# Paged attention: half of the pages fetched by rows on GpSimd, transposes alternating between two pairs of banks, and the prompt's value sums of two heads interleaved

## The chip, the cores and the metric

The kernel runs on one core of one Trainium2 chip. The metric is the device time in microseconds of one execution; before the change the median of three runs is 2847.95 us (2846.03 to 2848.89). TensorE is called PE, VectorE DVE, ScalarE ACT, GpSimd POOL and SyncE SP in the profile. Everything is computed in float32.

## What is computed

The reference is one inference step of a two-layer decoder trunk, for a prompt of 1024 tokens and 8 sample sequences of 4 new tokens each (32 tokens), with a mixture of experts after each layer. The first layer holds a gated convolution and a recurrent block, the second a convolution module and a latent attention with 8 heads. The change lies in that attention. With keys and values in one latent of 256 numbers per position and a rotary key of 32, the reference is

```
s = einsum('bthr,bsr->bhts', q_lat, ckv) + einsum('bthp,bsp->bhts', q_pe, kpe)
s = where(k_pos <= q_pos, s * SCALE, -inf)
p = softmax(s)                      # over the positions s
o_lat = einsum('bhts,bsr->bthr', p, ckv)
y = einsum('bthr,rhv->bthv', o_lat, w_uv)
```

For the prompt, s runs over 1024 positions, causally. For a sample sequence it runs over 4096 past positions, which lie in a cache as 32 pages of 128 rows in an order given by a page table, and over its 4 new positions. A cache row is 288 numbers: 256 of the latent and 32 of the rotary key, 1152 bytes.

## The kernel before

Every engine has its own program, written out by hand, and the programs meet only in semaphores; each engine runs its instructions in the written order. The stages follow one another: first layer, experts, second layer's projections (`*_odd`), prompt attention (`*_prompt`), paged attention (`*_sample`), output projection, experts.

**Prompt attention.** Heads go in pairs: two iterations of a loop with two pairs (`a`, `pp`), so four rounds. A round projects queries, keys and values of a pair (lines 1263 to 1275) and then works through 16 units u = 2t + j: block t of 128 queries, head j of the pair. `scores(u)` multiplies against (t+1)·128 keys, into PSUM banks 0/1 or 2/3 by the parity of u. DVE masks and takes the maximum (`maximum`), ACT takes the exponential (`expo`), DVE divides (`divide`), PE transposes the t+1 blocks of the probabilities into banks 4/5 (`turn`), ACT copies these to SBUF (`stage`; one place for each head, the tiles cosq and sinq), and `weigh(u)` multiplies them with the values (line 1253). The output of head 0 lies in PSUM partitions 0 to 63, that of head 1 in 64 to 127, of bank 6 or 7 by the parity of t. PE's order in step u is scores(u+1), turn(u-1), weigh(u-2). One product of 128·128 with 128·64 is one `matmul` in the source and two instructions in the profile.

**Paged attention.** There are two places for pages, `kv[0]` (the tile xT) and `kv[1]`; sequence b lies in place s = b mod 2. SP loads a sequence as four quarters h of 8 pages. For each page it reads the physical page number from the table and issues one DMA of 128 rows (`load_quarter`, lines 1384 and 1385). The semaphore d_pv, which PE raises after each quarter of the old sequence has been weighed, frees a quarter's place, and SP waits for it at line 1403.

`body(b, s)` on each engine does the scores of sequence b and finishes sequence b-1 between them. There are ten turns for a sequence. Turns 0 and 5 transpose the rotary keys of half the pages, which POOL has copied together (`rotary_keys`, line 1562; it waits for both quarters of its half). Turns 1 to 4 and 6 to 9 transpose four pages each, eight transposes into PSUM banks 0 and 1; ACT copies bank 0 and DVE bank 1 to SBUF (`take`, lines 1595 and 1646). Turn k waits until both copies of turn k-1 are done (lines 1437 and 1438). PE's order in a body is: turns 0 and 1, the transpose of the row maxima (1477), turn 2, the matmul that spreads the bias (1482), turns 3 and 4, the eight transposes of the probabilities of b-1 (1493, also into banks 0 and 1) and their sums, scores(0), turn 5, weigh(0), turn 6, weigh(1), turn 7, weigh(2), turn 8, weigh(3), turn 9, and scores(4). The scores go to banks 2/3 or 4/5 by s. Each weigh is 8 pages. POOL's order is: for each later sequence, wait for the scores, fill the queries, and then the two rotary copies of its halves (`both`).

Before the first body PE waits for two weights and forms the latent queries of all sequences (lines 1416 to 1425, banks 3 to 5), ACT and DVE copy them out, and DVE spreads the rotary queries (lines 1629 to 1636).

**Gathers elsewhere.** POOL gathers rows with indirect DMAs in the experts (line 726, 128 rows of 2 KB; the index column is copied first, line 722) and in the FFN's end (line 876, 128 rows of 4 KB).

Of the kernel before, what the change touches and what calls it, by code (L numbers as in the profile page):

```python
# [53 lines left out]
C_ID, C_ONE, C_TRI, C_IOTA, C_IOTA4, C_TOK, C_VALID, C_CAUSAL, C_NEW, C_FOLD, C_ROW, C_LOW, C_HALF, C_N = 0, 128, 256, 384, 400, 404, 422, 431, 559, 815, 943, 1071, 1199, 1200  # L54
# [27 lines left out]
def build(nc, io):  # L82
    ctx = contextlib.ExitStack()
    with ctx:
# [59 lines left out]
        pages = sb("pages", [1, SEQS * PAGES], I32)  # L144
        with contextlib.ExitStack() as st:
# [17 lines left out]
            with contextlib.ExitStack() as st2:  # L163
# [9 lines left out]
                nmax, nms, den, rden = (sb(n, [P, 2]) for n in ("nmax", "nms", "den", "rden"))  # L173
# [799 lines left out]
        def sp_odd(sp):  # L973
            w_in = io["w_in_odd"].rearrange("(k p) n -> p k n", p=P)
            for dst, src in ((odp[:], io["od_pack"]), (gqk[:], io["gqk"]), (cosq[:], io["cosq"]), (sinq[:], io["sinq"]),
                             (wuv[:], io["wuv"].rearrange("(k p) n -> p k n", p=P)), (pages[:], io["page_table"])):
                sp.dma_start(dst, src).then_inc(sem("in_odd"), 16)
# [151 lines left out]
        def dve_odd(dve, D):  # L1129
# [94 lines left out]
        def pe_prompt(pe):  # L1224
# [22 lines left out]
            def weigh(u, u0, t0):  # L1247
                t, j = divmod(u, 2)
                pe.wait_ge(sem("a_pt"), 1 + u0 + u + 1)
                if j == 0:  # L1250
                    pe.wait_ge(sem("a_yt"), t0 + t + 1)
                for b in range(t + 1):
                    ins = nc.tensor.matmul(PS[V_DIM * j:V_DIM * (j + 1), 6 + t % 2, 0:P], V[:, b, V_DIM * j:V_DIM * (j + 1)], PT[u % 2][:, b, :],  # L1253
                                           start=(b == 0), stop=(b == t))
                ins.then_inc(sem("a_v"), 1)

            with pe.Fori(0, 2) as a:
                for pp in range(2):
# [19 lines left out]
                    for u in range(18):  # L1278
                        if u + 1 < 16:
                            scores(u + 1, u0)  # L1280
                        if 0 <= u - 1 < 16:
                            turn(u - 1, u0)
                        if 0 <= u - 2 < 16:
                            weigh(u - 2, u0, t0)

        def act_prompt(act, A):
# [18 lines left out]
            def result(t, a, pp, u0):  # L1305
                act.wait_ge(sem("a_v"), u0 + 2 * t + 2)
# [73 lines left out]
        ROUND = [1, 2, 3, 4, 6, 7, 8, 9]  # L1380

        def load_quarter(sp, b, s, h):
            for n in range(h * 8, h * 8 + 8):
                phys = sp.value_load(pages[0:1, bass.ds(b * PAGES + n, 1)], min_val=0, max_val=io["cache"].shape[0] // PAGE - 1)  # L1384
                sp.dma_start(page(s, n), io["cache"][bass.ds(phys * PAGE, PAGE), :]).then_inc(sem(f"in_kv{s}{h}"), 16)  # L1385
# [5 lines left out]
        def sp_sample(sp):  # L1391
            for h in range(4):
                load_quarter(sp, 0, 0, h)
# [4 lines left out]
            for h in range(4):  # L1398
                load_quarter(sp, 1, 1, h)
            with sp.Fori(0, 3) as i:  # L1400
                for s in range(2):
                    for h in range(4):
# [12 lines left out]
        def pe_sample(pe):  # L1415
            pe.wait_ge(sem("in_attn_w"), 64)

            for r in range(2):
                for h in range(HEADS):
                    ins = nc.tensor.matmul(PS[:, 4 + r, h * SAMPLE:(h + 1) * SAMPLE], wukT[h // 4][:, h % 4, r * P:(r + 1) * P], qns[:, h, :], start=True, stop=True)  # L1420
            ins.then_inc(sem("d_ql"), 1)

            for r in range(2):
                ins = nc.tensor.transpose(PS[0:SAMPLE, 3, r * P:(r + 1) * P], ckvT[:, r, PROMPT:TOK], ident)
            ins.then_inc(sem("d_ql"), 1)

            def body(b, s, first, last):
                sb_ = 2 + 2 * s

                def turn(k):  # L1430
# [6 lines left out]
                    pe.wait_ge(sem("d_cta"), b * 10 + k)  # L1437
                    pe.wait_ge(sem("d_ctd"), b * 10 + k)
                    part(pe)
                    if q is None:  # L1440
                        for n in range(4):
                            ins = nc.tensor.transpose(PS[:, n // 2, n % 2 * P:n % 2 * P + P], kpr[:, k // 5, n, :, :].rearrange("p a b -> p (a b)"), ident)
                    else:
                        for n in range(8):
                            ins = nc.tensor.transpose(PS[:, n // 4, n % 4 * P:n % 4 * P + P], page(s, 4 * q + n % 4)[:, n // 4 * P:(n // 4 + 1) * P], ident)  # L1445
                    ins.then_inc(sem("d_t"), 1)

                def scores(q0):
# [3 lines left out]
                    bank = sb_ + q0 // 4  # L1452
# [25 lines left out]
                if not last:  # L1478
                    turn(2)
                if not first:  # L1480
# [6 lines left out]
                if not first:  # L1487
                    pe.wait_ge(sem("d_e"), b * 2)
                    if not last:
                        pe.wait_ge(sem("d_cta"), b * 10 + 5)  # L1490
                        pe.wait_ge(sem("d_ctd"), b * 10 + 5)
                    for n in range(8):
                        nc.tensor.transpose(PS[:, n // 4, n % 4 * P:n % 4 * P + P], Pd[:, n * P:(n + 1) * P], ident)
# [54 lines left out]
        def pool_sample(pool):  # L1548

            CP = nc.gpsimd.tensor_copy  # L1550
            pool.wait_ge(sem("d_ql"), 1)
# [24 lines left out]
            with pool.Fori(0, 3) as i:  # L1576
                for s in range(2):
                    pool.wait_ge(sem("d_s"), i * 4 + 2 * s + 2)
                    part(pool)
                    fill(i * 2 + 2 + s, s)  # L1580
                    both(i * 2 + 2 + s, s)

        def act_sample(act, A):
            AC = nc.scalar.activation
            act.wait_ge(sem("d_ql"), 1)
            act.wait_ge(sem("d_qp"), 1)
            for r in range(2):
                src = PS[:, 4 + r, 0:HEADS * SAMPLE].rearrange("p (h b t) -> p b h t", h=HEADS, t=STEP)
                AC(qlat[:, r, :, :].rearrange("p b (h t) -> p b h t", t=STEP), src, ACT.Copy).then_inc(sem("d_qa"), 1)

            def body(b, s, first, last):
                def take(k):
                    act.wait_ge(sem("d_t"), b * 10 + k + 1)
                    part(act)
                    ins = AC(CT[ROUND.index(k) % 4][:, 0, :], PS[:, 0, :], ACT.Copy) if k in ROUND else \
# [307 lines left out]
```

## Time and profile before

| | us |
|---|---|
| median of three runs | 2847.95 |
| the profiled execution | 2847.57 |
| its span, first to last instruction | 2845.8 |
| prompt attention, a round (four) | 64.85 |
| paged attention, scores(0) of one sequence to scores(0) of the next | 44.3 to 45.4 |

| engine | busy us | share of the span |
|---|---|---|
| PE | 2343.5 | 82% |
| DVE | 980.7 | 34% |
| ACT | 610.5 | 21% |
| POOL | 325.4 | 11% |

A row of the timeline gives the start in us from the span's start, the duration (of several merged instructions from the first start to the last end), the engine, the line, the operation, output and inputs, partitions and elements, the count, and in brackets how long the engine had been idle and what released it. "issue" means that nothing in the profile explains the idle time. PE's ends are modelled, so start times are read rather than ends. Tiles are shown by the name of the memory: cosq and sinq are the transposed probabilities of the two heads, lngb the probabilities, peT and CT the turned pages, KT the turned rotary keys. The clock column is the granted TensorE clock: 1.00 is 2.4 GHz and 0.50 is 1.2 GHz. DMA is the mean busy share of the 16 DMA engines, and the last number is GB/s.

### The profile page before, as it was taken

To read this page: it belongs to the slowest core of one execution; us is meant where nothing else is said; L and a number is where in the kernel's file an instruction comes from. 1 tells how busy PE (TensorE), PEld (TensorE's weight loads), DVE (VectorE), ACT (ScalarE), POOL (GpSimd) and SP (SyncE) were. 2 spreads that over 40 slices of the span, in tenths; PEclk is the share of its full clock that TensorE was granted. 3 is DMA by queue.
4 is the path that set the end of the run, shared out by engine and by line. 5 is a ranking of instruction groups with operands and counts; after the bars stand their busy time and mean duration, and the time that the engine had idled before them with its cause. 6 is when DMAs were issued, how large, how long until landed. Compare 5 with 4: busy or idle time off the path is not lost.

```text
span 2845.8 us, 41210 instructions
## 1 busy us (share of the span) xinstructions
PE 2343.5 (82%) x13984; PEld 1388.1 (49%) x13985; DVE 980.7 (34%) x1711; ACT 610.5 (21%) x1037; POOL 325.4 (11%) x362
## 2 busy tenths in 40 slices
PE   7999798599999934979799987676897798999850
PEld 4666454355555523645466664444454454555420
DVE  2333333311111154798855442222233311111117
ACT  2222211111111122321344432111111110111112
POOL 0000000000100042742000000000000000001014
PEclk9999899699999966989988887766898799999985
DMA  3112223167677665102000122334424158555845
GB/s 118 38 38 89 87 99 140 59 233 288 230 260 275 221 190 165 37 26 83 22 6 26 46 68 73 100 103 113 146 71 162 32 219 304 219 207 172 306 144 184
DMA packets 175229, 384.45 MB, mean 135 GB/s; under 512 B 16241, under 2 KB 89346, under 8 KB 175154
## 3 DMA queue, kind: packets, MB, share of 16 engines
q1 hardware_dynamic: 146882, 314.31, 31.3%
q0 software_dynamic: 13072, 44.88, 4.9%
q10 hardware_dynamic: 15200, 24.39, 3.2%
q8 instruction: 31, 0.51, 0.1%
q14 instruction: 44, 0.36, 0.0%
HBM read 339.18 MB, written 44.35 MB: 135 GB/s over the span
## 4 chain that ended last, share of the span: by engine, by line
PE 68%; DVE 17%; DMA 4%; issue 4%; SPq 3%; ACT 1%; DVEq 1%; POOL 0%; ACTq 0%; POOLq 0%
PE PS L770 20%; PE PS L783 11%; PE PS L292 10%; PE PS L505 9%; DVE yT L241 5%; PE PS L1237 3%; PE PS L1445 2%; PE PS L1253 2%; DMA w<-in_w_exp_out 2%; DVE yst L241 2%; SPq L1384 2%; SPq L1385 1%; PE PS L778 1%; PE PS L1244 1%; PE PS L1455 1%
## 5 line engine op out<-in xcount | busy, mean ns | idle before, releaser
L770 PE MATMUL PS<-yT,yst 128*64 128x256 f32 x2816 | 315.7, 383 | 22.3 <-DMA w<-in_w_exp_out 22.3
L783 PE MATMUL PS<-w,ht 128*64 128x512 f32 x1312 | 317.8, 605 | 11.5
L292 PE MATMUL PS<-xT,W 128*128 128x352 f32 x960 | 287.8, 463 | 18.1 <-ACTq L301 18.1
L770 PE MATMUL PS<-xT,yst 128*64 128x256 f32 x2432 | 275.0, 385 | 19.2 <-DMA w<-in_w_exp_out 10.7
L770 PEld LDWEIGHTS PS<-yT,yst 128*64 128x64 f32 x2816 | 204.3, 139 | 145.5 <-issue 52.8
L505 PE MATMUL PS<-wo,yst 128*128 128x512 f32 x576 | 257.9, 603 | 17.3 <-POOL yst L483 15.4
L292 PEld LDWEIGHTS PS<-xT,W 128*128 128x128 f32 x960 | 184.2, 192 | 120.1 <-ACTq L301 17.8
L770 PEld LDWEIGHTS PS<-xT,yst 128*64 128x64 f32 x2432 | 177.8, 139 | 127.5 <-issue 47.1
L998 PE MATMUL PS<-xT,W 128*128 128x352 f32 (+1 forms) x672 | 203.2, 466 | 33.7 <-ACT qT L1073 21.6
L998 PEld LDWEIGHTS PS<-xT,W 128*128 128x128 f32 (+1 forms) x672 | 127.2, 190 | 109.5 <-issue 45.4
L505 PEld LDWEIGHTS PS<-wo,yst 128*128 128x128 f32 x576 | 108.8, 193 | 142.7 <-issue 142.7
L817 ACT ACTIVATE sg<-PS 128x128 f32<-128x128 f32 x164 | 45.4, 277 | 592.8 <-PE PS L770 592.4
L833 DVE TENSOR_TENSOR hx<-sg,PS 128x128 f32<-128x128 f32 x164 | 46.4, 283 | 340.1 <-ACT sg L817 340.1
L241 DVE SCALAR_TENSOR_TENSOR yT<-hp,odp,yT x88 | 153.2, 1741 | 16.0 <-DVE yT L241 15.2
L837 DVE COPY ht<-PS 128x128 f32<-128x128 f32 x164 | 47.8, 292 | 321.0 <-PE PS L778 321.0
L726 POOL DMA_INDIRECT yst<-xm,idx x84 | 81.3, 968 | 555.4 <-PE PS L755 544.6
L783 PEld LDWEIGHTS PS<-w,ht 128*64 128x64 f32 x1312 | 79.6, 136 | 121.9 <-issue 70.2
L846 DVE COPY wo<-PS 128x512 f32<-128x512 f32 x82 | 56.7, 692 | 207.9 <-PE PS L783 207.9
L488 PE MATMUL PS<-cst,xn 128*128 128x128 f32 x216 | 38.3, 336 | 82.2 <-POOL xn L887 69.6
L817 ACT ACT_TABLE_LOAD x38 | 48.8, 1283 | 240.4 <-issue 240.4
L1237 PE MATMUL PS<-K,Q 96*128 96x512 f32 (+3 forms) x192 | 90.4, 588 | 7.4 <-ACT lngb L1297 4.5
L584 DVE SCALAR_TENSOR_TENSOR sx<-xres,PS 128x1024 f32<-128x1024 f32 x18 | 22.0, 1221 | 177.8 <-PE PS L505 177.8
(335 smaller groups left out, 2666.8 us busy)
## 6 DMA issues: line engine op xcount, KB each, us to landing
xT<-in_w_exp_in SPq DMA_DIRECT2D x32, 2048.0 KB, 12.8
w<-in_w_exp_out SPq DMA_DIRECT2D x32, 2048.0 KB, 18.2
yT<-in_w_exp_in SPq DMA_DIRECT2D x32, 2048.0 KB, 12.8
yb<-wo ACTq DMA_DIRECT2D x164, 128.0 KB, 2.3
xT<-in_cache SPq DMA_DIRECT2D x128, 144.0 KB, 2.1
kv<-in_cache SPq DMA_DIRECT2D x128, 144.0 KB, 2.1
W<-in_w_in_even SPq DMA_DIRECT2D x20, 512.0 KB, 4.0
xm<-xn SPq DMA_DIRECT2D x18, 512.0 KB, 2.9
```

The source lines that it names most:

```text
L241: return nc.vector.scalar_tensor_tensor(out, x, scalar, acc, ALU.mult, ALU.add)
L292: ins = nc.tensor.matmul(PS[:, n % 5, 0:CW], W5[:, p, k, :], xT[:, k, c * CW:(c + 1) * CW], start=(k == 0), stop=(k == KD - 1))
L505: ins = nc.tensor.matmul(PS[:, (t % 2) * 2 + n, :], yst[:, s, k, :], wo[:, k, n * 512:(n + 1) * 512], start=(k == 0), stop=(k == KD - 1))
L726: pool.indirect_dma_start(out=gx, out_offset=None, in_=xm[l].rearrange("t (h c) -> (t h) c", h=2), in_offset=bass.IndirectOffsetOnAxis(ap= ...
L770: ins = nc.tensor.matmul(PS[cols, 2 + q, 0:2 * P].rearrange("p (g f) -> p g f", g=2), xtb[:, k, :], w[:, k, t, :, q * P:(q + 1) * P], star ...
L783: ins = nc.tensor.matmul(PS[cols, 4, :], ht[:, q, t, :], w2[:, s, 2 * t + q, n * 512:(n + 1) * 512], start=(q == 0 and t == 0), stop=(q == ...
L817: nc.scalar.activation(sg[:, q, :], PS[:, 2 + q, 0:P], ACT.Silu).then_inc(sem(u + "sg"), 1)
L998: ins = nc.tensor.matmul(PS[0:m, (n0 + c) % 6, 0:CW], W4[:, slot, k, 0:m], xT[:, k, c * CW:(c + 1) * CW], start=(k == 0), stop=(k == KD - 1))
L1237: ins = nc.tensor.matmul(PS[:, u % 2 * 2 + c // 512, 0:w], Q[j][:, t * P:(t + 1) * P], K[j][:, c:c + w], start=True, stop=True)
L1253: ins = nc.tensor.matmul(PS[V_DIM * j:V_DIM * (j + 1), 6 + t % 2, 0:P], V[:, b, V_DIM * j:V_DIM * (j + 1)], PT[u % 2][:, b, :], start=(b = ...
L1384: phys = sp.value_load(pages[0:1, bass.ds(b * PAGES + n, 1)], min_val=0, max_val=io["cache"].shape[0] // PAGE - 1)
L1445: ins = nc.tensor.transpose(PS[:, n // 4, n % 4 * P:n % 4 * P + P], page(s, 4 * q + n % 4)[:, n // 4 * P:(n // 4 + 1) * P], ident)
```

## The change

It has three parts.

- **Pages.** The page table is loaded into all 128 partitions, and DVE turns it, at the start of the second layer, into row numbers: page·128 + partition. SP loads quarters 0 and 2 as before. POOL fetches quarters 1 and 3: it copies 8 columns of the row numbers and issues 8 indirect DMAs, each of which gathers 128 rows. In the loop POOL does so after it has filled the queries and before the two rotary copies (`both`). At the start it gathers sequence 0 when the projections have read xT, and sequence 1 when the last prompt result is written, ahead of its first rotary copy.
- **Banks.** Turn k writes banks 0/1 or 4/5 by the parity of k and waits for the copies of turn k-2. The probabilities are transposed into banks 4/5. The scores of both places go to banks 2/3. The latent queries are formed after turn 2 of the first body, in banks 6 and 7, and DVE's rotary queries come after its second copy there.
- **Prompt.** `weigh` takes a block t of both heads at once, alternating between the heads, in the odd steps, ahead of turn(u-1).

Its core (the query part moves as said; ACT and DVE read the new banks):

```diff
-        pages = sb("pages", [1, SEQS * PAGES], I32)
+        pages = sb("pages", [P, SEQS * PAGES], I32)
+        pidx = sb("pidx", [P, 32], I32)
...
+            D(nc.vector.tensor_copy(rtmp[:, 0:SEQS * PAGES], pages[:, :]))
+            D(TS(rtmp[:, 0:SEQS * PAGES], rtmp[:, 0:SEQS * PAGES], float(PAGE), cst[:, C_PART:C_PART + 1], ALU.mult, ALU.add))
+            D(nc.vector.tensor_copy(pages[:, :], rtmp[:, 0:SEQS * PAGES]))
             dve.sem_inc(sem("o_zero"), 1)
...
-            def weigh(u, u0, t0):
-                t, j = divmod(u, 2)
-                pe.wait_ge(sem("a_pt"), 1 + u0 + u + 1)
-                if j == 0:
-                    pe.wait_ge(sem("a_yt"), t0 + t + 1)
+            def weigh(t, u0, t0):
+
+                pe.wait_ge(sem("a_pt"), 1 + u0 + 2 * t + 2)
+                pe.wait_ge(sem("a_yt"), t0 + t + 1)
                 for b in range(t + 1):
-                    ins = nc.tensor.matmul(PS[V_DIM * j:V_DIM * (j + 1), 6 + t % 2, 0:P], V[:, b, V_DIM * j:V_DIM * (j + 1)], PT[u % 2][:, b, :],
-                                           start=(b == 0), stop=(b == t))
+                    for j in range(2):
+                        ins = nc.tensor.matmul(PS[V_DIM * j:V_DIM * (j + 1), 6 + t % 2, 0:P], V[:, b, V_DIM * j:V_DIM * (j + 1)], PT[j][:, b, :],
+                                               start=(b == 0), stop=(b == t))
...
+                        if u >= 3 and u % 2 == 1:
+                            weigh((u - 3) // 2, u0, t0)
                         if 0 <= u - 1 < 16:
                             turn(u - 1, u0)
-                        if 0 <= u - 2 < 16:
-                            weigh(u - 2, u0, t0)
...
+        PAIR = [0, 4]
...
+        def gather_quarter(pool, b, s, h):
+
+            j = s * 16 + h // 2 * 8
+            nc.gpsimd.tensor_copy(pidx[:, j:j + 8], pages[:, bass.ds(b * PAGES + h * 8, 8)]).then_inc(sem("d_ix"), 1)
+            pool.wait_ge(sem("d_ix"), b * 2 + h // 2 + 1)
+            part(pool)
+            for n in range(8):
+                pool.indirect_dma_start(out=page(s, h * 8 + n), out_offset=None, in_=io["cache"],
+                                        in_offset=bass.IndirectOffsetOnAxis(ap=pidx[:, j + n:j + n + 1].bitcast(U32), axis=0)
+                                        ).then_inc(sem(f"in_kv{s}{h}"), 16)
...
             with sp.Fori(0, 3) as i:
                 for s in range(2):
-                    for h in range(4):
+                    for h in (0, 2):
                         sp.wait_ge(sem("d_pv"), i * 8 + (4 * s + h + 1))
                         load_quarter(sp, i * 2 + s + 2, s, h)
...
-                    pe.wait_ge(sem("d_cta"), b * 10 + k)
-                    pe.wait_ge(sem("d_ctd"), b * 10 + k)
+                    if not first or k >= 2:
+                        pe.wait_ge(sem("d_cta"), b * 10 + k - 1)
+                        pe.wait_ge(sem("d_ctd"), b * 10 + k - 1)
                     part(pe)
+                    bank = PAIR[k % 2]
...
                 if not last:
                     turn(2)
+                if first:
+                    queries()
...
         def pool_sample(pool):
-            pool.wait_ge(sem("d_ql"), 1)
+            pool.wait_ge(sem("o_zero"), 1)
+            pool.wait_ge(sem("o_mm"), 1 + 9 + 42)
+            for h in (1, 3):
+                gather_quarter(pool, 0, 0, h)
+            pool.wait_ge(sem("a_yt"), 2 + 32)
+            pool.wait_ge(sem("a_qns"), 8)
+            for h in (1, 3):
+                gather_quarter(pool, 1, 1, h)
...
                     fill(i * 2 + 2 + s, s)
+                    for h in (1, 3):
+                        pool.wait_ge(sem("d_pv"), i * 8 + (4 * s + h + 1))
+                        gather_quarter(pool, i * 2 + s + 2, s, h)
                     both(i * 2 + 2 + s, s)
```

## Rows read from the trace of the kernel before

**Rows 1.** Stretches: length, busy us (instructions) PE, PEld, DVE, ACT, POOL; clock, DMA.

```profile
1476.96:1541.81 64.85, 61.66 (x323) 41.75 (x323) 31.66 (x85) 29.27 (x60) 0.00 (x0) 0.92 0.02 6
1625.50:1634.50 9.00, 9.00 (x24) 4.73 (x23) 4.57 (x15) 3.54 (x10) 0.00 (x0) 0.50 0.00 0
1780.00:1825.90 45.90, 31.21 (x272) 20.68 (x268) 10.14 (x23) 7.76 (x16) 1.66 (x4) 0.69 0.38 104
1799.50:1825.50 26.00, 15.95 (x68) 11.06 (x72) 5.86 (x16) 4.87 (x10) 1.66 (x4) 0.50 0.42 115
```

**Rows 2.** Timeline, one sequence: start, us, engine, line, operation, count, idle before.

```profile
1782.57 1.07 PE L1465 MATMUL PS<-kv,lngb 128*32 128x256 f32 x16
1784.52 37.57 SPq L1385 DMA_DIRECT2D kv<-in_cache  x32
1804.93 0.61 POOL L1562 COPY kpr<-kv 128x512 f32<-128x512 f32 x1 [25.07 <-DMA kv<-in_cache]
1805.79 1.09 PE L1442 MATMUL PS<-cst,kpr 128*128 128x128 f32 x4 [10.72 <-POOL kpr L1562]
1808.70 0.15 DVE L1658 TENSOR_TENSOR mxd<-mxd,mxn 32x1 f32<-32x1 f32 x1
1819.13 1.94 PE L1493 MATMUL PS<-cst,lngb 128*128 128x128 f32 x8 [0.99 <-DVE peT L1646]
1822.18 1.07 PE L1455 MATMUL PS<-CT,qb 128*32 128x512 f32 x2
```

**Rows 3.** A row of the chain; then the timeline of a round's end.

```profile
1603.41 3.26 PE PS L1253 x32
...
1594.94 1.98 PE L1237 MATMUL PS<-K,Q 96*128 96x512 f32 x4
1600.75 1.02 ACT L1303 ACTIVATE cosq<-PS 128x1024 f32<-128x1024 f32 x1 [0.64 <-PE PS L1244]
1604.81 0.27 PE L1253 MATMUL PS<-cosq,V 128*64 128x128 f32 x1
1604.87 0.27 PE L1253 MATMUL PS<-sinq,V 128*64 128x128 f32 x1
1606.60 5.59 PE L1263 MATMUL PS<-qT,wqn 128*128 128x352 f32 x18
```

**Rows 4.** Timeline of GpSimd, first FFN stage: index copy and gathers.

```profile
531.86 0.19 POOL L722 COPY idx<-table 128x1 int32 x1 [94.30 <-issue]
533.00 1.01 POOL L726 DMA_INDIRECT yst<-xm,idx  x1 [0.95 <-POOL idx L722]
...
1022.64 0.99 POOL L876 DMA_INDIRECT wo<-yb,dest  x1 [7.61 <-DMA yb<-wo]
1028.95 0.94 POOL L876 DMA_INDIRECT wo<-yb,dest  x1 [0.30 <-issue]
1032.02 1.80 POOL L876 DMA_INDIRECT wo<-yb,dest  x1 [2.13 <-DVE sx L241]
```

**Rows 5.** Timeline from the prompt's end to the second sequence.

```profile
1666.88 6.58 DVE L1634 COPY qpz<-peT 32x32 f32<-32x32 f32 x32
1671.71 0.28 ACT L1308 ACTIVATE yT<-PS 128x128 f32 x1 [2.23 <-PE PS L1253]
1676.88 7.03 PE L1420 MATMUL PS<-qns,lngb 64*128 64x32 f32 x32 [5.36 <-DMA lngb<-in_wukT]
1684.83 1.09 PE L1442 MATMUL PS<-cst,kpr 128*128 128x128 f32 x4 [0.38 <-POOL kpr L1562]
1698.77 1.07 PE L1455 MATMUL PS<-CT,qb 128*32 128x512 f32 x2 [0.98 <-DVE peT L1646]
1703.72 0.66 PE L1442 MATMUL PS<-cst,kpr 128*128 128x128 f32 x4
1707.38 1.07 PE L1445 MATMUL PS<-cst,xT 128*128 128x128 f32 x8 [1.11 <-DVE CT L1646]
1716.47 0.66 PE L1442 MATMUL PS<-cst,kpr 128*128 128x128 f32 x4
```

More of the change, by code:

```diff
@@ L172, in build @@
                 PT = [x[:, 0:PROMPT].rearrange("p (a b) -> p a b", b=P) for x in (cosq, sinq)]
-                nmax, nms, den, rden = (sb(n, [P, 2]) for n in ("nmax", "nms", "den", "rden"))
+                smx = sb("smx", [P, 8])
+                nmax, nms, den, rden = (smx[:, 2 * n:2 * n + 2] for n in range(4))
         with contextlib.ExitStack() as st:
@@ L1391, in sp_sample @@
         def sp_sample(sp):
-            for h in range(4):
+            sp.wait_ge(sem("o_zero"), 1)
+            for h in (0, 2):
                 load_quarter(sp, 0, 0, h)
@@ L1397, in sp_sample @@
                 sp.dma_start(wukT[n], io["wukT"][:, 4 * n:4 * n + 4, :]).then_inc(sem("in_attn_w"), 16)
-            for h in range(4):
+            for h in (0, 2):
                 load_quarter(sp, 1, 1, h)
@@ L1401, in sp_sample @@
                 for s in range(2):
-                    for h in range(4):
+                    for h in (0, 2):
                         sp.wait_ge(sem("d_pv"), i * 8 + (4 * s + h + 1))
@@ L1415, in pe_sample, with queries @@
         def pe_sample(pe):
[L1416 to L1425, printed above, removed]
+            def queries():
+                pe.wait_ge(sem("in_attn_w"), 64)
+                for r in range(2):
+                    for h in range(HEADS):
+                        ins = nc.tensor.matmul(PS[:, 6, (r * HEADS + h) * SAMPLE:(r * HEADS + h + 1) * SAMPLE], wukT[h // 4][:, h % 4, r * P:(r + 1) * P], qns[:, h, :], start=True, stop=True)
+                ins.then_inc(sem("d_ql"), 1)
+                for r in range(2):
+                    ins = nc.tensor.transpose(PS[0:SAMPLE, 7, r * P:(r + 1) * P], ckvT[:, r, PROMPT:TOK], ident)
+                ins.then_inc(sem("d_ql"), 1)
             def body(b, s, first, last):
-                sb_ = 2 + 2 * s
                 def turn(k):
@@ L1584, in act_sample, with queries @@
             AC = nc.scalar.activation
[L1585 to L1589, printed above, removed]
+            def queries():
+                act.wait_ge(sem("d_ql"), 1)
+                for r in range(2):
+                    src = PS[:, 6, r * HEADS * SAMPLE:(r + 1) * HEADS * SAMPLE].rearrange("p (h b t) -> p b h t", h=HEADS, t=STEP)
+                    AC(qlat[:, r, :, :].rearrange("p b (h t) -> p b h t", t=STEP), src, ACT.Copy).then_inc(sem("d_qa"), 1)
             def body(b, s, first, last):
@@ L1601, in body @@
                     take(2)
+                if first:
+                    queries()
                 if not first:
                     act.wait_ge(sem("d_nm"), b)
-                    AC(Pd[:, :].rearrange("p (a b) -> p a b", a=2), PS[:, 4 - 2 * s:6 - 2 * s, :], ACT.Exp, scale=SCALE, bias=nmd[:, :], accum_out=dend[:, :]).then_inc(sem("d_e"), 1)
+                    AC(Pd[:, :].rearrange("p (a b) -> p a b", a=2), PS[:, 2:4, :], ACT.Exp, scale=SCALE, bias=nmd[:, :], accum_out=dend[:, :]).then_inc(sem("d_e"), 1)
                     AC(Pn[:, :], sn[:, :], ACT.Exp, scale=SCALE, bias=nmd[0:QS, :], accum_out=denn[:, :]).then_inc(sem("d_e"), 1)
@@ L1660, in body @@
                     take(1)
+                if first:
+                    rotary_queries()
                 if not first:
@@ L1666, in body @@
                     take(2)
+                if first:
+                    new_keys()
                 if not first:
@@ L1689, in body @@
                     take(9)
-            with D.rounds(0, 1, 1):
+            with D.rounds(0, 1 + 33 + 1, 1):
                 body(0, 0, True, False)
@@ L1809, in constants @@
     c[:, C_HALF] = np.arange(P) >= BLK
+    c[:, C_PART] = np.arange(P)
     c[:, C_VALID:C_VALID + NT] = tok < TOK
```

60 lines of the change are left out of this document (31 added, 29 removed).

## The prediction

> **What bounds the kernel now.** The change touches two stages in the middle: prompt attention (four rounds, 1412 to 1671.5 us) and paged attention over eight sequences (1671.5 to 2036). I read the busy times by stage first, then the timeline of one round and of one sequence.
>
> A prompt round lasts 64.85 us, of which TensorE (PE) is busy 61.66, VectorE 31.66 and ScalarE 29.27 [rows 1]: it is PE-bound. The reader should also see its granted clock, 0.92, and the 9 us with PE fully busy at 0.50, the lower level (1.2 GHz) [rows 1].
>
> In a sequence (45.9 us, PE busy 31.2) [rows 1] nothing is saturated; it is a loop through the page loads. weigh(0) of the old sequence ends at 1782.57 + 1.07 = 1783.64. SyncE then issues 32 pages in 37.57 us, 1.17 each [rows 2]. The first rotary copy on GpSimd, which wants quarters 0 and 1, starts at 1804.93 after 25.07 us idle behind that DMA; turn 0 follows at 1805.79, 22.15 us after the weigh. From there to scores(0) at 1822.18 the five turns and the transposes of the probabilities go one at a time through one pair of banks: 16.39 us. The transposes of Pd (line 1493) start at 1819.13, 13.34 after turn 0, after a wait for VectorE's copy, and scores(0) starts 3.05 later [rows 2].
>
> **The change, part by part.**
>
> *Prompt value sums.* A block of one head is two instructions; 32 of them took 3.26 us, 0.204 us a block [rows 3]. The two heads write different halves of the output partitions. Where the old order lets their edges meet, cosq and sinq start 0.06 us apart (1604.81, 1604.87) instead of about 0.10 [rows 3], so alternated they run at about double rate: 0.054 an instruction. For t = 1 to 5 that removes 2+3+4+5+6 = 20 blocks of 0.204 = 4.1 us a round; the five blocks of t = 1 and 2 ran at clock 0.50 [rows 1] and count twice: 5.1. I give nothing for t = 0, where PE waits for the softmax chain.
>
> Nothing for t = 6 and 7 either: no weigh is left to cover ScalarE's copy out of PSUM (1.02 us for eight blocks). Before, from scores(15) at 1594.94 to the next projection at 1606.60: 11.66 us [rows 3]. After, in PE's order: scores 1.8, seven transposes 0.9 (eight take 1.07 [rows 5]), copy 1.1, weigh 28 x 0.054 = 1.5, transposes 1.1, copy 1.2, transposes 1.1, copy 1.2, weigh 1.7: 11.6. The gain there pays for three waits. Such pauses can also bring the clock down, which I price at 0.6 a round (estimate; a weigh of 1.7 doubled and half of a projection would be about 4). Sum: 4 x (5.1 - 0.6) = **-18 us**, bounds 0 (every saving lost to the copy) and -29 (all 36 blocks, 7.3 a round).
>
> *Pages by gather.* SyncE keeps quarters 0 and 2: 16 x 1.17 = 18.8 us. GpSimd gets 1 and 3. The nearest rows are the FFN's gathers, also 128 rows each: six in a row start at 1022.64 to 1028.95, one per 1.26 us, 0.94 busy; one whose start meets a VectorE operation on SBUF takes 1.80. A copy of indices takes 0.19, and the gather starts 0.95 after it [rows 4]. A quarter is 0.19 + 0.95 + 7 x 1.26 + 0.94 = 10.9.
>
> What matters is what is queued behind: the program order on GpSimd is quarter 1, quarter 3, then the rotary copies. So the first copy, which wants only quarters 0 and 1, stands behind quarter 3. From weigh(0): weigh(1) ends 2.1 later (a turn and a weigh of 1.07 each), two quarters 21.8, gaps 0.6 (two as between gathers), copy 0.61, release 0.25: turn 0 at 25.4 instead of 22.15, **+3.2 us a sequence**, although half of the issuing has left SyncE. Ends: without the 0.32 between gathers 16 x 0.32 = 5.1 less, -1.9; with 1.80 each, 16 x 0.86 = 13.8 more, +17. I take 1.26: six starts in a row on a quiet VectorE. The second copy needs quarter 3 landed; turn 5 comes after scores(0), over 12 us after turn 0, which hides it.
>
> The Trainium skill (SBUF — State Buffer, the section on the two sides and their ports) says that VectorE and GpSimd share a port pair under an exclusive lock, so that a VectorE operation in its two-port mode keeps GpSimd from writing descriptors. The 1.80 row beside 0.94 agrees. In the sequence stage VectorE mostly reads PSUM and is busy 10.14 of 45.9 us [rows 1], so by that rule few gathers should be held; were it all of them, the +17 above.
>
> *Two pairs of banks.* Turn k no longer waits for the copies of turn k-1. At clock 0.50 eight transposes take 1.94 [rows 2]. New walk from turn 0: turn 0 to 1.1, turn 1 to 3.0; VectorE's maxima end at 3.06 as before (1808.70 + 0.15 - 1805.79); their transpose (0.4) to 3.6; turn 2 to 5.5; the bias matmul to 6.1; turns 3 and 4 to 10.0; Pd there instead of at 13.34: **-3.3 to -3.8 us**, I take -3.5. The exponentials are not last: before, the wait ahead of Pd ended with VectorE's copy [rows 2], and they start from the same bias matmul. I count nothing for the clock: granted 0.50 holds from 1799.5 to 1825.5, all of the turns and most of scores(0) [rows 1], and turn 0 still follows over 10 us of idle PE. The second half gains nothing, turns and weighs already alternate there without a gap; at the end nothing is turned. Net 3.2 - 3.5 = -0.3, six times for sequences 2 to 7: **-2 us**; scores in one pair of banks cost nothing, as the exponentials have read it before scores(0) (they precede Pd).
>
> *Start of the sample stage.* GpSimd now starts sequence 1's gathers when the last prompt result is written (1671.71 + 0.28), before it copies the keys of sequence 0: 21.8 + 0.3 + 0.3 + 0.61 + 0.25 puts turn 0 at 1695.2 instead of 1684.83. The query projections (7.03 us, plus 0.6 of transposes) no longer stand in front but after turn 2; VectorE's rotary queries (0.9 + 6.58) lie beside them. Turns 0 to 2 end at 1700.2, the queries at 1707.8, turns 3 and 4 and the last copy at 1712.3: scores(0) there instead of 1698.77, 13.5 late [rows 5]. Turns 5 to 9, at the full clock, had four waits for copies, one of them the 1.11 in the row, all but one of that size [rows 5]; those go: -4.2. So body 1 starts 9 us late (was 1716.47), and its own turns give back 3: **+6 us**, bounds 0 (its turns at the full clock) and +15 (GpSimd slower).
>
> *Hidden.* The three index operations on VectorE come before ScalarE's first use of a projection and cost well under 2 us; the broadcast page table is one small DMA among six. Sequence 0's sixteen gathers run some 250 us early; they begin beside VectorE's last operations before the prompt, and should one of these be held by a gather it costs 0.94. Fewer pages on SyncE help no one here.
>
> **Sum** against the profiled execution, 2847.57 (span 2845.8; the median of the runs is 2847.95): -18 - 2 + 6 = -14, so 2833.6; I say **2834**.
>
> **Rivals.**
>
> *Slower: gathers dearer than in the FFN.* They sit 112 deep on the path (6 x 16, and 16 at the start), all ahead of the rotary copies. At 0.125 us more each the gain is gone, above 0.18 the kernel is measurably slower. If a quarter of them take 1.80, as one that met VectorE did [rows 4]: 28 x 0.86 = +24, 2858; if all, 2930. For it: VectorE copies eight banks in the first 10 us after the weigh. Against: these read PSUM. A sharing of the DMA engines is of the same kind: they are 0.38 to 0.42 busy in this stage [rows 1], and the gathers nearly double the rate. Chance 0.15.
>
> *No change: the prompt gains nothing*, since PE waits for the copies in every pair of units and not only in the last two: -2 + 6 = +4, 2852. For it: the copy lost its cover. Against: in the middle of a round scores of 0.9 (half of the row for eight blocks) to 1.8 us follow each turn and last as long as the copy. Chance 0.13.
>
> *Much faster: the denser turns bring the clock back before scores(0).* A turn then takes 1.07 [rows 5] instead of 1.94; three such groups and half of scores(0)'s 5.0 (1698.77 to 1703.72): 5 us a sequence, -30, 2804. Against: the 16 us of turns now, PE mostly busy, stay at 0.50. A gather of 1.0 us would give about the same. Chance 0.12.
>
> **How the numbers follow.** The forecast has 0.60, by itself 2820 to 2848. A measurement can tell about 0.2% (5.7 us). Faster: 0.54 of the forecast's 0.60 and the 0.12 of the last rival, 0.66; the same: 0.06 of the forecast and 0.13, 0.19; slower: 0.15. The range takes in the first price of the slow rival and part of the fast one: 2811 to 2857.
>
> **What would show it.** Rounds of about 60.5 us with value matmuls 0.054 apart, and PE waiting for the PSUM copy in the last units; on GpSimd sixteen gathers 1.26 apart, the rotary copy right behind the last and no longer behind a DMA; turn 0 about 25 us after weigh(0); Pd's transposes 10 us after turn 0; body 1's turn 0 about 9 us later against the prompt's end. Wrong if gathers are spaced well away from 1.26, if PE waits in mid-round, or if the clock in the turns leaves 0.50.

## The result and the profile after

| | before | after | ratio (95% interval) |
|---|---|---|---|
| median of runs, us | 2847.97 | 2785.18 | 0.9778 [0.9764, 0.9791] |
| range of runs, us | 2846.03 to 2848.89 | 2782.7 to 2785.93 | |
| span of the profiled execution, us | 2845.8 | 2781.0 | |

The change makes the kernel 63 us faster. The prediction had the direction, and under a quarter of the size: -14, with a range that ended at 2811. One execution of the last run below took 10562 us where its other five took 2712 to 2716; its median leaves that one out.

The two spans, cut at the same events, show where the 64.8 us went:

| stretch | before, us | after, us | difference |
|---|---|---|---|
| start to the first prompt projection | 1406.4 | 1405.7 | -0.7 |
| four prompt rounds, to the last result's copy | 265.3 | 236.8 | -28.5 |
| prompt's end to scores(0) of sequence 1 | 59.84 | 60.94 | +1.1 |
| scores(0) of sequence 1 to scores(0) of sequence 7 | 269.26 | 233.72 | -35.5 |
| from there to the next projection | 37.32 | 35.80 | -1.5 |

The last 800 us (output projection and second FFN) did not move. So two terms make the result, and both were forecast too small: the prompt (-18 forecast) and the six sequences in the loop (-2 forecast).

The busy times of three stretches of the kernel after follow. The columns are as in [rows 1]. The first is the prompt round that answers to its first row, the second the low part of one sequence, the third what comes right behind it.

```profile
1467.56:1526.19 58.63, 52.21 (x323) 33.76 (x323) 31.42 (x85) 28.65 (x60) 0.00 (x0) 0.91 0.02 7
...
1724.00:1737.50 13.50, 4.79 (x21) 4.07 (x21) 2.77 (x9) 0.98 (x2) 7.36 (x11) 0.50 0.44 134
1738.00:1761.50 23.50, 19.18 (x237) 12.37 (x236) 7.10 (x14) 6.26 (x14) 8.78 (x11) 1.00 0.40 116
```

The reader should see two things. The round is 6.2 us shorter, and PE's busy time fell by more, 9.45. And the stretch at the granted clock 0.50 (1.2 GHz) ends at about 1737.4 (0.58 in the half microsecond up to 1737.5, 1.00 in the next), in the middle of the turns; in the kernel before it went on until 1825.5, to nearly the end of scores(0) [rows 1].

The timeline of that sequence, to be held against [rows 2]:

```profile
1706.71 1.07 PE L1483 MATMUL PS<-xT,lngb 128*32 128x256 f32 x16
1708.71 18.80 SPq L1392 DMA_DIRECT2D xT<-in_cache  x16
1710.01 0.19 POOL L1397 COPY pidx<-pages 128x8 int32 x1 [14.56 <-PE PS L1483]
1711.01 0.97 POOL L1401 DMA_INDIRECT xT<-in_cache,pidx  x1 [0.81 <-POOL pidx L1397]
1712.28 0.95 POOL L1401 DMA_INDIRECT xT<-in_cache,pidx  x1 [0.30 <-issue]
...
1730.58 0.95 POOL L1401 DMA_INDIRECT xT<-in_cache,pidx  x1 [0.30 <-issue]
1731.53 0.62 POOL L1589 COPY kpr<-xT 128x512 f32<-128x512 f32 x1
1732.39 1.09 PE L1460 MATMUL PS<-cst,kpr 128*128 128x128 f32 x4 [13.18 <-POOL kpr L1589]
1733.27 1.91 PE L1463 MATMUL PS<-cst,xT 128*128 128x128 f32 x8
1737.83 1.97 PE L1463 MATMUL PS<-cst,xT 128*128 128x128 f32 x16
1740.56 1.09 PE L1513 MATMUL PS<-cst,lngb 128*128 128x128 f32 x8 [0.76 <-ACT peT L1625]
1742.34 0.62 PE L1473 MATMUL PS<-CT,qb 128*32 128x512 f32 x2
1745.07 0.66 PE L1460 MATMUL PS<-cst,kpr 128*128 128x128 f32 x4
```

The gathers are what was forecast: 1.25 us from start to start, the copy of the keys (1731.53) right behind the sixteenth, turn 0 at 1732.39, which is 24.6 us after weigh(0) ended at 1707.78 (22.15 before, 25.4 forecast). What was not forecast is what follows. Turn 1 still takes 1.91; turns 3 and 4 together take 1.97, eight transposes in half the time. From turn 0 to scores(0) it is 9.95 us (16.39 before, 12.9 by the prediction's walk; 9.1 to 10.9 in the other five sequences), and scores(0) to turn 5 takes 2.73 instead of 4.70. A sequence takes 38.95 us on average instead of 44.88.

### The profile page after: what moved, and what is told of

Same layout as the page of the kernel before. It is cut to its first block, busy times and chain, and to the rows that moved or that the text cites. A ratio compares the mean times of both kernels' runs of the same rounds, so it can differ in the third digit from the quotient of the medians.

```text
span 2781.0 us, 40569 instructions
## 1 busy us (share of the span) xinstructions
PE 2255.3 (81%) x13984; PEld 1327.2 (48%) x13985; DVE 980.6 (35%) x1714; ACT 607.0 (22%) x1037; POOL 454.4 (16%) x506
## 3 DMA queue, kind: packets, MB, share of 16 engines
q1 hardware_dynamic: 128592, 295.56, 29.5%
## 4 chain that ended last, share of the span: by engine, by line
PE 67%; DVE 17%; issue 5%; POOL 4%; DMA 4%; ACT 2%; DVEq 1%; SPq 0%; ACTq 0%; POOLq 0%
PE PS L772 20%; PE PS L785 11%; PE PS L294 10%; PE PS L507 9%; DVE yT L243 6%; PE PS L1243 2%; DMA w<-in_w_exp_out 2%; POOL kv L1401 2%; DVE yst L243 2%; POOL xT L1401 1%; PE PS L1259 1%; PE PS L1250 1%; PE PS L1463 1%; PE PS L780 1%; PE PS L520 1%
## 5 line engine op out<-in xcount | busy, mean ns | idle before, releaser
L724 POOL COPY idx<-table 128x1 int32 x84 | 15.5, 184 | 513.5 <-DMA yst<-xm,idx 325.3
L1460 PE MATMUL PS<-cst,kpr 128*128 128x128 f32 x64 | 13.7, 352 | 103.5 <-POOL kpr L1589 103.5
```

## The experiments

Each run's time is set against 2785 (the changed kernel) and against its own runs of the kernel before, which lie between 2846.9 and 2849.6. Theory: *the two pairs of banks make PE's work in the turns unbroken enough that the clock comes back early, and the overlapped copies are the smaller part.* Rivals: the gathers do it; the overlap alone does it; the prompt's gain is not the edit's own.

**One pair of banks.** Everything of the change but the second pair.

```diff
-        PAIR = [0, 4]
+        PAIR = [0, 0]
...
-                    if not first or k >= 2:
-                        pe.wait_ge(sem("d_cta"), b * 10 + k - 1)
-                        pe.wait_ge(sem("d_ctd"), b * 10 + k - 1)
+                    pe.wait_ge(sem("d_cta"), b * 10 + k)
+                    pe.wait_ge(sem("d_ctd"), b * 10 + k)
...
```

> The changed kernel with one pair of banks for all turns, each turn waiting for the copies of the turn before; gathers and prompt as changed. Theory (it was the denser turns that brought TensorE's clock back to 1.00 before scores(0)): the level stays 0.50 until after scores(0), turn 0 to scores(0) is 16.4 us again, a sequence 44.8 + 2.4 = 47.3 us: 2785 + 6 x 8.3 + 6 at the start = 2841. Rival (the clock comes back for another reason, such as the shorter first half of the sequence or the later turn 0): turn 0 to scores(0) about 13 us, a sequence of about 42, 2803.

Measured: 2856.23, ratio to before 1.0025 [1.0015, 1.0035]: a quarter of a per cent slower than the kernel before, although the prompt's gain is in it. Its stretches, and the first PE rows of a sequence:

```profile
1791.00:1821.00 30.00, 17.63 (x100) 12.44 (x100) 5.86 (x16) 4.87 (x10) 7.63 (x11) 0.50 0.19 58
1799.61:1816.00 16.39, 12.63 (x52) 10.23 (x53) 4.92 (x13) 4.27 (x9) 1.09 (x3) 0.50 0.02 6
```

```profile
1801.37 1.94 PE L1462 MATMUL PS<-cst,kv 128*128 128x128 f32 x8 [0.68 <-DVE KT L1682]
...
1812.94 1.94 PE L1512 MATMUL PS<-cst,lngb 128*128 128x128 f32 x8 [0.99 <-DVE peT L1681]
1816.00 1.07 PE L1472 MATMUL PS<-CT,qb 128*32 128x512 f32 x2
```

Turn 0 to scores(0) is 16.39 us, to the digit what it was before the change, all of it at 0.50. A sequence takes 48.29 us, 3.4 more than before: that is the price of the gathers without the second pair (3.2 forecast). The theory expected 2841. Of the 15 us beyond it some 9 are at the start, where sequence 1's turns fell to 0.50 too: its scores(0) comes 75.5 us after the prompt's end instead of 60.9, which is 14.5 where 6 was expected. The other 6 are a microsecond more in each of the six sequences (48.29, 47.3 expected). The rival, that the clock comes back for another reason, is out.

**One pair of banks, and work for nothing.** As above, with four transposes of the identity ahead of the waits of turns 1 to 4.

```diff
+                    if 1 <= k <= 4:
+                        for _ in range(4):
+                            nc.tensor.transpose(PS[:, 4, 0:P], ident, ident)
                     pe.wait_ge(sem("d_cta"), b * 10 + k)
...
```

> As the run with one pair of banks, and ahead of the wait of each of turns 1 to 4 PE does four transposes of the identity into a bank that nobody reads: 16 instructions more per sequence, no work less. Theory (the clock follows how unbroken PE's work is, whatever the work is for): the level is back at 1.00 within turns 2 to 4 and scores(0) runs at it; 4 to 7 us a sequence less than with one pair alone, about 2805 to 2817. Rival (useful turns that overlap their copies are what counts; filler only adds): the level stays 0.50, the run is the same as with one pair or up to 12 us slower.

Measured: 2808.56, 48 us faster than the run above, which does 16 instructions a sequence less. The timeline of one sequence, then two of its stretches:

```profile
1742.83 1.06 PE L1455 MATMUL PS<-cst 128*128 128x128 f32 x4
1743.71 1.94 PE L1465 MATMUL PS<-cst,xT 128*128 128x128 f32 x8
...
1746.60 1.07 PE L1465 MATMUL PS<-cst,xT 128*128 128x128 f32 x8
...
1750.72 1.06 PE L1465 MATMUL PS<-cst,xT 128*128 128x128 f32 x8 [0.62 <-ACT peT L1627]
1752.78 1.07 PE L1515 MATMUL PS<-cst,lngb 128*128 128x128 f32 x8 [0.99 <-DVE peT L1684]
```

```profile
1743.00:1746.50 3.50, 3.50 (x18) 3.03 (x16) 2.38 (x8) 0.98 (x2) 1.05 (x3) 0.53 0.01 2
1747.00:1754.50 7.50, 5.85 (x46) 4.82 (x43) 2.14 (x4) 3.17 (x7) 0.00 (x0) 1.00 0.01 2
```

The first turn of pages takes 1.94, the second 1.07: the level went from 0.50 to 1.00 between them, in a stretch in which PE has no gap. The waits for copies are still there (0.62, 0.99), yet turn 0 to scores(0) is 12.57 us, and a sequence 41.77. So of the 9.34 us a sequence that the second pair of banks brings (48.29 to 38.95), 6.52 come with the clock alone and the overlap adds 2.82. That is the split with the clock taken first and with what the filler itself may cost in it; no run has the overlap at the low level. The prediction priced the overlap at 3.5 and the clock at nothing.

**No gathers.** SyncE loads all four quarters again; the pairs of banks and the prompt stay (in `sp_sample` the loops over `(0, 2)` become `range(4)`, and the calls of `gather_quarter` go).

> The changed kernel with all four quarters loaded by SyncE again, no gathers. Theory (the two pairs of banks bring the clock back, whoever fetches): turns 0 to 4 still run at 1.00 towards their end and scores(0) starts about 10 us after turn 0. Turn 0 comes at about 22 us after the old weigh(0) instead of 24.6. But SyncE's 32 loads last 37.6 us and quarter 3 lands some 40 us after weigh(0), so turn 5 waits for it, where it started 37.3 us after weigh(0): a sequence of 42 to 43 us instead of 38.95, +20 for six, some 7 back at the start: about 2800. Rival (SyncE's loads stay hidden behind the turns as in the kernel before): a sequence of 36.5 us, 2761. Second rival (the gathers, not the banks, brought the clock back): the level stays 0.50 until after scores(0), a sequence of about 42 us too, but with PE at 0.50 there: told apart by the clock rows.

Measured: 2794.09, ratio 0.9806 [0.979, 0.9823]. The gathers did not bring the clock back: without them it is back before scores(0) as well (0.81 on the mean from turn 0 to scores(0), which takes 9.25 us). But the loads are now last:

```profile
1750.70:1759.95 9.25, 8.17 (x52) 7.02 (x52) 4.91 (x13) 4.04 (x9) 0.00 (x0) 0.81 0.42 118
...
1749.84 0.61 POOL L1585 COPY kpr<-kv 128x512 f32<-128x512 f32 x1 [23.84 <-DMA kv<-in_cache]
1750.70 1.08 PE L1460 MATMUL PS<-cst,kpr 128*128 128x128 f32 x4 [9.70 <-POOL kpr L1585]
...
1769.28 0.61 POOL L1585 COPY kpr<-kv 128x512 f32<-128x512 f32 x1 [18.82 <-DMA kv<-in_cache]
1770.10 1.09 PE L1460 MATMUL PS<-cst,kpr 128*128 128x128 f32 x4 [7.35 <-issue]
```

PE is idle for 7.35 us ahead of turn 5 (1770.10), until the copy of the second half's keys (1769.28), which waited for SyncE's DMA. A sequence takes 44.3 us from sequence 2 on. So the gathers cost 3.4 us a sequence in the kernel with one pair and bring 5.3 in the kernel with two. In all they are worth only 9 us there, because they cost 26 at the start: without them scores(0) of sequence 1 comes 34.6 us after the prompt's end, with them 60.9. The expectation had 7 for that.

**The prompt's edit alone**, in the kernel before.

> The kernel before with the new value sums of the prompt alone: once per pair of units, the two heads alternated; pages, banks and the start of the sample stage as before. Theory (the shorter prompt stage of the changed kernel, 28.5 us over four rounds, is this edit's alone): 2848 - 28.5 = 2819.5, and with the changed kernel at 2785 some 34 us are left for the sample stage. Rival (the price of the prediction, 18 us, was right, and the rest of the shorter rounds comes from elsewhere, such as SyncE's lighter queue): 2830.

Measured: 2818.99, ratio 0.9902 [0.9888, 0.9916], -27.9 us. The theory is right to half a microsecond, and with 2785 the sample stage has the remaining 34.

**Heads one after the other.** In the changed kernel the two loops of the sum are swapped.

```diff
-                for b in range(t + 1):
-                    for j in range(2):
+                for j in range(2):
+                    for b in range(t + 1):
```

> The changed kernel, with the prompt's value sums still issued once per pair of units, but all blocks of one head and then all of the other. Theory (the whole prompt gain is the overlap of the two heads' matmuls): by the chains, the eight sums of a round take 18.7 us head after head (the kernel before) and 9.9 alternated; the new place leaves all of that on PE's path, so rounds of 58.6 become about 67 and the kernel 2785 + 4 x 8.8 = 2820, more than the prompt stage ever gained. Rival (a good part of the gain is the new order, one sum per pair of units, with fewer switches between kinds of work): rounds of 60 to 63 us, 2790 to 2802.

Measured: 2798.5, ratio 0.982 [0.9803, 0.9836]: 13 us back, not 35. The theory fails, the rival holds. The rows of the chain of waits show why: first the kernel before (two sums of t = 4, one for each head), then this run and the changed kernel (one sum for both, t = 5). The columns are start, length, what, and instructions.

```profile
1517.37 1.24 PE PS L1253 x10
...
1520.97 1.24 PE PS L1253 x10
```

```profile
1516.86 2.38 PE PS L1259 x24
```

```profile
1506.12 1.24 PE PS L1259 x20
...
1512.05 1.46 PE PS L1259 x24
```

From 20 to 24 instructions the alternated sum grows by 0.22, 0.055 an instruction. Before, t = 4 cost 2.48 for both heads and t = 5 2.91 (1.45 and 1.46 in the same view); issued back to back the two sums of t = 5 take 2.38, since at the seam the second head starts under the first; alternated 1.46. By the same views each of t = 2 to 5 is 0.53 shorter back to back than before. Of the 28 us nearly half is the alternation itself (13), and the rest comes with issuing both heads' sums together.

**The clock while PE waits.** In sequences 2, 4 and 6, 80 transposes of the identity in PE's idle time before turn 0.

> The changed kernel; in sequences 2, 4 and 6 PE does 80 transposes of the identity (10.7 us at the full clock) while it waits for the rotary copy, and in 1 as well, where it delays turn 0; 3, 5 and 7 are left as they are. Theory (the clock already comes back in time, what is left below 1.00 in turns 0 to 2 is hidden by the exponentials): in 2, 4 and 6 the level stays 1.00, and scores(0) starts about 8.8 us after turn 0, as in sequence 1, instead of 9.1 to 10.9: under 1 us a sequence, and the delay in sequence 1 costs 10: 2790 to 2795. Rival (the low level in turns 0 to 2 is still on the path in full): scores(0) 6.5 to 7 us after turn 0, 2.5 us a sequence.

Measured: 2784.19 in one execution, no difference, and no answer: the filler was shorter than planned (8.97 us, 10.7 expected). (It is not in sequence 1; the expectation had that wrong.) Stretches of sequence 2:

```profile
1720.23:1729.20 8.97, 8.95 (x84) 8.71 (x80) 0.00 (x0) 0.00 (x0) 6.32 (x9) 1.00 0.75 224
1733.40:1737.50 4.10, 3.78 (x17) 3.19 (x18) 2.67 (x9) 0.98 (x2) 1.05 (x3) 0.50 0.10 31
```

The 80 ran at 1.00, 0.112 us each, and ended 4.2 us ahead of turn 0; by then the level was 0.50 again.

**The copy between the gathers.** The prediction had remarked that the first copy stands behind gathers that it does not need. Here it comes earlier.

```diff
-        def gather_quarter(pool, b, s, h):
+        def gather_quarter(pool, b, s, h, lo=0, hi=8):
...
-                    for h in (1, 3):
-                        pool.wait_ge(sem("d_pv"), i * 8 + (4 * s + h + 1))
-                        gather_quarter(pool, i * 2 + s + 2, s, h)
-                    both(i * 2 + 2 + s, s)
+                    bb = i * 2 + s + 2
+                    pool.wait_ge(sem("d_pv"), i * 8 + (4 * s + 2))
+                    gather_quarter(pool, bb, s, 1)
+                    pool.wait_ge(sem("d_pv"), i * 8 + (4 * s + 4))
+                    gather_quarter(pool, bb, s, 3, 0, 2)
+                    pool.wait_ge(sem("d_t"), bb * 10 + (-9))
+                    rotary_keys(bb, s, 0)
+                    gather_quarter(pool, bb, s, 3, 2, 8)
+                    pool.wait_ge(sem("d_t"), bb * 10 + (-4))
+                    rotary_keys(bb, s, 1)
```

> The changed kernel, and in the loop over sequences GpSimd makes the first rotary copy after quarter 1's gathers and two of quarter 3's, and the other six gathers after it. Theory (turn 0 is late because the copy that it needs stands behind gathers that it does not need): in the changed kernel's second sequence the copy would start at 1724.3 instead of 1731.53, so turn 0 comes 7.2 us earlier in each of sequences 2 to 7: 2785 - 43 = 2742. Rival (quarter 3 then becomes last: its gathers end only 0.6 us earlier or later than before, they take 3.4 us to land, and turn 5 waits for the second copy): the first half gains 7, the second loses 2 to 5 again, 2755 to 2772. Rival 2 (turn 0 gets another bound, the pages that SyncE loads): no change, 2785.

Measured: 2740.91, ratio 0.9621 [0.9605, 0.9637]; the theory said 2742.

```profile
1725.95 0.95 POOL L1402 DMA_INDIRECT xT<-in_cache,pidx  x1 [0.30 <-DMA xT<-in_cache,pidx]
1726.91 0.61 POOL L1590 COPY kpr<-xT 128x512 f32<-128x512 f32 x1
1727.69 0.97 POOL L1402 DMA_INDIRECT xT<-in_cache,pidx  x1 [0.17 <-issue]
1727.77 1.08 PE L1461 MATMUL PS<-cst,kpr 128*128 128x128 f32 x4 [5.67 <-POOL kpr L1590]
```

Turn 0 follows the copy while the gathers go on; PE's wait is 5.67 us instead of 13.18. The second copy does not become last: nothing in PE's waits names it.

**The start in another order.** GpSimd copies both halves of sequence 0's keys first, then gathers quarter 1 of sequence 1, fills the query tiles, and gathers quarter 3.

> The changed kernel, and at the start of the sample stage GpSimd copies both halves of sequence 0's keys first, then gathers quarter 1 of sequence 1, fills the query tiles, and gathers quarter 3. Theory (the 22 us between the prompt's end and turn 0 are nothing but sequence 1's gathers ahead of sequence 0's copy): turn 0 about 2 us after the prompt's end instead of 22.6, scores(0) at about 19 instead of 38.1 (behind the query projections and the fill), the next sequence's turn 0 at about 33 instead of 52.1: 2785 - 19 = 2766. Rival (the queries bound the start: their weights land late and VectorE's rotary queries take 6.6 us): scores(0) at 28 or later, 2776.

Measured: 2761.42, ratio 0.969 [0.9674, 0.9706], 24 us less than the changed kernel. Turn 0 comes 1.2 us after the prompt's end, scores(0) at 16.7, sequence 1's turn 0 at 29.5 (52.1 in the changed kernel): the theory, and a little better. The queries were not the bound.

**Both orders.**

> The edits of the two runs before (copy between the gathers, and the new order at the start) in one kernel. Theory (the two places are independent): the sum of both gains, 2785 - 43 - 19 = 2723. Rival (the second rotary copy or SyncE's loads become the bound in the loop): 2736 to 2753.

Measured: 2716.86, ratio 0.9536 [0.952, 0.9552]. They add.

**A filler that fits.** On top of both orders, in sequences 2, 4, 6 and 7; the waits for the copies move ahead of it.

```diff
+                    if k == 0 and not first and (s == 0 or isinstance(b, int)):
+                        for _ in range(46):
+                            nc.tensor.transpose(PS[:, 0, 0:P], ident, ident)
...
```

> The kernel with the new copy order and the new start, and in sequences 2, 4, 6 and 7 PE does 46 transposes of the identity (5.2 us by the 80 that took 8.95) in the 5.7 us in which it waits for the rotary copy. Theory (what is left below 1.00 in turns 0 to 2 costs little): the level stays 1.00 there, turn 0 to scores(0) becomes 8.8 instead of 9.2 to 10.8, 3 to 4 us in all: 2713. Rival (turns 0 to 2 count in full, 2.5 us a sequence): 2707. Rival 2 (the filler ends after the copy and holds turn 0 back): 2718 to 2722.

Measured: 2711.43, ratio 0.9524 [0.9512, 0.9536]. Turn 0 to scores(0) with the filler (sequence 2) and without it (sequence 3), in the same execution:

```profile
1702.59:1711.35 8.76, 6.81 (x53) 5.76 (x53) 4.91 (x13) 4.04 (x9) 5.70 (x6) 1.00 0.62 182
1732.70:1742.72 10.02, 8.94 (x53) 7.60 (x53) 4.91 (x13) 4.04 (x9) 6.31 (x7) 0.75 0.54 157
```

Between these two it is 1.26 us. Against the run of both orders, sequence by sequence, it is 0.5 to 2.1 (9.67, 9.39, 9.24 and 10.79 there; 8.76, 8.77, 8.76 and 8.69 here), 4.1 in all: the theory (3 to 4) holds, and the rival's 2.5 a sequence does not. At 1.00 PE's busy time falls by 2.1, and 0.8 of it turns into a longer wait for VectorE's maxima (1.1 us instead of 0.3, by the waits of the two stretches). The gain in the total is 5 us; the two ratios' intervals overlap.

**The end of a prompt round.** On top of both orders, unit 14 is transposed into banks 0 and 1, ahead of the sum of t = 6, and its copy waits for that sum.

> The kernel with the new copy order and the new start, and at the end of each prompt round the transposes of unit 14 go into banks 0 and 1, ahead of the value sum of t = 6, so that they no longer wait for the copy of unit 13; the copy of unit 14 waits for that sum. Theory (PE's three waits for the copies at a round's end are on the path in full, and one of them goes with the transposes behind it): 1.6 us a round, 2717 - 6.5 = 2710. Rival (the softmax of unit 14 is not ready that early, or the clock falls in what is left of the pause): no change, 2717.

Measured: 2717.43, ratio 0.9542 [0.953, 0.9555]: nothing. The chain of waits at a round's end, then the stretch of the sum of t = 6:

```profile
1520.97 0.77 DVE lngb L1360
...
1521.79 1.09 PE PS L1251 x8
1522.88 3.18 PE PS L1260 x28
```

```profile
1522.88:1526.06 3.18, 3.18 (x29) 2.85 (x30) 0.22 (x1) 0.00 (x0) 0.00 (x0) 0.50 0.01 5
```

Both halves of the rival are there. The transposes of unit 14 wait for its softmax on VectorE until 1521.79 (PE is idle for 1.94 us), and behind that pause the sum of t = 6 takes 3.18 us at 0.50, where the changed kernel took 1.75; it is 2.92 to 3.21 in all four rounds. What the order gave, the clock took.

**Everything together.**

> The edits of the two kernels before in one, on the new copy order and the new start. Theory (they lie in different stages and add): 2717 - 4 - 6.5 = 2706. Rival: one of the two gives nothing, 2710 to 2713.

Measured: 2714.0 (the median of five), ratio 0.9534 [0.9522, 0.9546], no better than without the prompt's end. The lowest time is that of the filler that fits, 2711; without any work for nothing it is both orders at 2717.

## Why the prediction was right and wrong

**The step that failed** is in the part on the two pairs of banks: "I count nothing for the clock: granted 0.50 holds from 1799.5 to 1825.5, all of the turns and most of scores(0) [rows 1], and turn 0 still follows over 10 us of idle PE." The row was read rightly and carried over wrongly. It describes turns with a wait of 0.4 to 1.0 us behind each, and these waits are just what the change removes. PE was busy 12.63 of 16.39 us in such turns (the run with one pair), and the level stayed at 0.50 through all of them; with the gaps filled, by the next turn or by work of no use, it rose within three turns. The idle time before turn 0 does bring the clock down, as the sentence says, but that settles only where the turns begin. Cost of the step: 6.5 us a sequence. The prediction's own rival, "the denser turns bring the clock back before scores(0)", names what happened, at 5 us a sequence; it got 0.12. The last of the prediction's own signs of being wrong, "if the clock in the turns leaves 0.50", is what came.

**The overlap of turns and copies** was priced at 3.5 us a sequence, at the low level, and added 2.8 at the high one.

**The gathers.** Near in every term: 1.25 us apart (1.26), a quarter in 10.7 (10.9), turn 0 at 24.6 us (25.4). Turn 0 comes 2.5 us later than before (3.2 forecast). That a sequence with one pair is 3.4 us longer, close to 3.2, is in part luck: about 0.5 of it lies in scores(0), where the level stays at 0.50 longer, and the forecast has no such term. The slow rival needed 0.18 us more for each; all 96 gathers of the loop took 0.94 to 0.97 us. The row of 1.80 [rows 4] met a VectorE instruction with two inputs in SBUF, which the profile does not show to be in a two-port mode. In the kernel after, gathers of sequence 0 took 1.99 and 2.03 us beside others with two inputs there, and 1.09 and 1.44 beside copies within SBUF. But "fewer pages on SyncE help no one here" was true only of the old pace. With the faster turns, SyncE's 32 loads would have been the bound.

**The prompt** was mis-sized: -18 against -28. The tail was worked out rightly: from scores(15) to the next projection 11.66 us before, 11.6 forecast, 11.77 after (1514.42 to 1526.19 in the round shown). Here are its last pieces in the chain of waits of the kernel after:

```profile
1514.42 1.72 PE PS L1243 x4
1516.14 0.78 PE PS L1250 x7
...
1516.95 0.93 ACT sinq L1309
...
1517.99 1.75 PE PS L1259 x28
...
1520.80 1.03 ACT cosq L1309
...
1523.07 1.03 ACT sinq L1309
...
1524.22 1.97 PE PS L1259 x32
1526.19 1.08 PE PS L1269 x3
```

Three copies now lie bare and pay for all that the last two sums gain. So the 6.2 us of this round came from its middle, where 5.1 was forecast. (The rival of no change is out: before this tail PE waits for no copy of ScalarE in the round.) The price of the old sums was taken from a row in which the two heads already overlap (3.26 us for 32, 0.102 an instruction, [rows 3]); in mid-round a sum of ten took 1.24. Nor did the clock cost the 0.6 a round that was set aside. This round spent as long at 0.50 as the round of [rows 1] did (clock 0.91 of 58.63 us, 0.92 of 64.85). The first and the third spent less (over the whole round 0.85 before and 0.89 after, and 0.92 and 0.94) and are 8.7 and 7.6 us shorter. Only the fourth, 6.0 shorter, shows what was set aside: behind the last copy its sum of t = 7 ran at 0.56 and took 3.44 us instead of 1.97. Why the clock fell there and not in the other three stays open.

**The start** was forecast at +6 and came at +1.1. Sequence 0's scores(0) is 11.0 us late against the prompt's end (13.5 forecast), sequence 1's turn 0 7.4 (9), and sequence 1's turns, at 1.00 all through, give back 6.3 where 3 was forecast: the same step again.

**By the Trainium skill** (TensorE: Matmul & The Clock Gate, "Part 4: PE-mode transpose") the full clock does not engage for transposes in TensorE's transpose mode; by that, turns filled with more of them should not have brought it back. The traces say otherwise: in the run with filler nearly all of PE's work from turn 0 on is transposes, and the second turn already takes 1.07. The trace lists them as ordinary matmuls with a 128x128 f32 operand; no run here shows whether that mode was on. Its "Part 3: Packing small matmuls — row/col tiling", by which matmuls in different columns of the array run at once, agrees with 0.055 us for an alternated instruction against 0.105 (1.24 to 1.45 us from ten to twelve) for one head alone.

## What to carry to other kernels

A granted clock read from the old trace belongs to the old gaps: where an edit closes the gaps in a stretch at the low level, work out the new stretch at both levels, and give the higher one a real chance. A copy or a gather has to stand in its engine's order right behind what it needs: moving one copy ahead of six gathers was worth 44 us here, more than the gathers themselves (9). And a bound that is hidden at the old pace (SyncE's loads) has to be priced again at the new one.

## What the runs showed of the hardware

Sixteen transposes a sequence whose output nobody reads made the kernel 48 us faster (2856 to 2809), by the clock alone. The reverse holds too: behind 1.94 us of idle PE and eight transposes at the end of a prompt round a sum ran at 0.50, 3.18 us for what took 1.75. And two f32 matmuls on different halves of the output partitions, issued in alternation, cost 0.055 us each where those of one half cost 0.105.
